# Compressed values on 32-row tiles of TensorE, and second score passes of two token blocks on separate 64-row halves

## What is computed

```
# first layer, sparse attention: 16 heads in 4 groups, head size 64; 31 compressed keys and values per group
s_c = einsum('bqgrd,bcgd->bgrqc', q, k_cmp) * scale + bias
p_c = masked_softmax(s_c, valid_c)
o_c = einsum('bgrqc,bcgd->bqgrd', p_c, v_cmp)
...
return gate0 * o_c + gate1 * o_s + gate2 * o_w      # selected and window parts beside it

# second layer, attention to the second memory: 4 heads of size 64, 256 memory tokens
sm = einsum('bshd,bmhd->bhsm', qm, km) * 64 ** -0.5
pm = softmax(sm)
o  = einsum('bhsm,bmhd->bshd', pm, vm)
```

## Time and profile before

| | |
|---|---|
| median of 3 runs | 2376.61 us (2376.5 to 2378.73) |
| span of the profiled execution | 2373.4 us |
| busy PE, PEld | 99%, 83% |
| busy DVE, ACT, POOL | 60%, 42%, 7% |
| chain that ended last | PE 96%, DVE 2%, ACT 1% |
| mean granted clock of TensorE | 0.998 |

### The profile page before, as it was taken

How to read it: one execution, slowest core, us unless ns; L and a number is a source line. 1 busy time by engine, 2 the same in 40 slices (tenths; PEclk the granted TensorE clock), 3 DMA queues, 4 the chain that set the end, 5 groups by cost and what they waited for, 6 DMA issues and landing times.

```text
span 2373.4 us, 30181 instructions
## 1 busy us (share of the span) xinstructions
PE 2350.3 (99%) x11448; PEld 1971.2 (83%) x11448; DVE 1420.6 (60%) x2891; ACT 1000.5 (42%) x1852; POOL 165.1 (7%) x251
## 2 busy tenths in 40 slices
PE   9999999999999999999999999999999999999998
PEld 7888889888888888878888888888888887888887
DVE  6434546775658897875434446677754667543444
ACT  4223335442335676653322234666523346322322
POOL 0000000110001223310000000111100001000000
PEclk9999999999999999999999999999999999999999
DMA  4455434332332211223333334211223432223322
GB/s 151 118 118 142 118 111 149 116 107 81 116 102 80 73 54 63 67 89 98 98 90 107 94 108 120 81 54 58 65 83 116 132 105 67 97 88 108 98 88 90
DMA packets 86410, 231.33 MB, mean 97 GB/s; under 512 B 8505, under 2 KB 23481, under 8 KB 86267
## 3 DMA queue, kind: packets, MB, share of 16 engines
q1 hardware_dynamic: 81072, 221.42, 29.5%
q10 hardware_dynamic: 5194, 7.98, 2.1%
HBM read 217.83 MB, written 11.53 MB: 97 GB/s over the span
## 4 chain that ended last, share of the span: by engine, by line
PE 96%; DVE 2%; ACT 1%; issue 1%; DMA 0%; POOL 0%; DVEq 0%; SPq 0%; ACTq 0%
PE bank L1136 92%; PE bank L1385 2%; PE bank L1211 1%; PE bank L1557 0%; PE bank L1232 0%; DMA t_XT<-in_xT 0%; DVE t_pp L2387 0%; DVE t_pw L2387 0%; ACT t_whi L1676 0%; DVE t_PS L2120 0%; DVE t_wlo L2115 0%; DVE t_XL L2124 0%; ACT t_pw L1829 0%; DVE t_XT L2765 0%; DVE t_PW L2120 0%
## 5 line engine op out<-in xcount | busy, mean ns | idle before, releaser
L1136 PE MATMUL bank<-t_XH,t_whi 128*128 128x512 f32 x2064 | 813.4, 394 | 0.7 <-DVE t_wlo L2115 0.5
L1136 PE MATMUL bank<-t_XL,t_whi 128*128 128x512 f32 x2064 | 804.7, 390 | 0.0
L1136 PE MATMUL bank<-t_XH,t_wlo 128*128 128x512 f32 x2048 | 799.0, 390 | 0.0
L2115 DVE TENSOR_TENSOR t_wlo<-t_raw,t_whi 128x1024 fp32r<-128x1024 f32 (+2 forms) x416 | 478.6, 1152 | 386.2 <-ACT t_whi L1676 382.8
L1676 ACT ACTIVATE t_whi<-t_raw 128x1024 fp32r<-128x1024 f32 (+3 forms) x422 | 416.9, 989 | 436.8 <-PE bank L1136 371.8
L1136 PEld LDWEIGHTS bank<-t_XH,t_whi 128*128 128x128 f32 x2064 | 388.0, 188 | 80.9 <-issue 1.6
L1136 PEld LDWEIGHTS bank<-t_XL,t_whi 128*128 128x128 f32 x2064 | 388.3, 188 | 77.1
L1136 PEld LDWEIGHTS bank<-t_XH,t_wlo 128*128 128x128 f32 x2048 | 384.8, 188 | 80.9
L1136 PE MATMUL bank<-t_RX,t_whi 128*128 128x512 f32 x1056 | 325.4, 390 | 0.0
L2243 DVE TENSOR_TENSOR t_tmp<-bank,t_RB 128x512 f32<-128x512 f32 x178 | 122.6, 689 | 198.6 <-PE bank L1136 193.3
L1136 PEld LDWEIGHTS bank<-t_RX,t_whi 128*128 128x128 f32 x1056 | 198.2, 188 | 41.0 <-issue 0.2
(11 more groups left out here) (335 smaller groups left out, 2686.9 us busy)
## 6 DMA issues: line engine op xcount, KB each, us to landing
t_raw<-in_f_in SPq DMA_DIRECT2D x86, 512.0 KB, 3.5
t_raw<-in_f_out SPq DMA_DIRECT2D x32, 384.0 KB, 3.1
t_raw<-in_w_conv SPq DMA_DIRECT2D x24, 512.0 KB, 3.5
t_raw<-in_w_merge SPq DMA_DIRECT2D x24, 512.0 KB, 3.5
t_raw<-in_fg SPq DMA_DIRECT2D x22, 512.0 KB, 3.4
t_raw<-in_fu SPq DMA_DIRECT2D x22, 512.0 KB, 3.4
t_raw<-in_f_out SPq DMA_DIRECT2D x32, 320.0 KB, 3.0
t_raw<-in_w_g SPq DMA_DIRECT2D x16, 512.0 KB, 3.5
```

The costliest lines, as they stand in the source:

```text
L1136: return e.matmul(o, l, r, start=start, stop=stop, skip_group_check=True)
L2115: e.tensor_tensor(wlo[n % NRAW][:, 0:width], raw[n % NRAW][:, 0:width], f32(whi[n % NHI][:, 0:width]), ALU.subtract).then_inc(*w_lo.tick(n))
```

## The change

1. **Compressed values.** `VC` becomes one 128-column piece: rows 32 r to 32 r + 31 hold head `r`'s values, without zeros around them. The four matmuls of a place use 32 rows each of `VC` and of `PCT`, and their order becomes: high part for both heads, then low part for both heads. The clearing of `VC` and the waits on it go.
2. **Stacked queries.** In odd blocks of tokens the halves are swapped: the high part lies in rows 64 to 127 and the low part in rows 0 to 63. `stack_q` writes even and odd blocks apart, so that each 64x512 piece becomes two pieces of 2x128 columns. This holds for all three kinds of heads.
3. **Score passes.** For `mm2` heads alone (`PAIRED`) an even tile's `score` issues only the first pass; the odd tile's `score` issues its own first pass and then both second passes, each on the 64 rows that hold the high part of the query, and a single update of the semaphore tells of both tiles. The `spa` and `win` tiles have the same passes on 128 rows as before.

```diff
+PAIRED = ('mm2',)
+def side(i):
+    return slice(64, 128) if i % 2 else slice(0, 64)
+def blocks(ap, odd):
+    return ap.rearrange("p (b o n) -> p b o n", o=2, n=P)[:, :, odd, :]
...
-    VC = place("VC", 18304, 512, F32R).rearrange("p (r n) -> p r n", r=4)
+    VC = place("VC", 18304, P, F32R)
...
         def score(t):
             hd, i = w.tiles[t]
...
+            if hd.kind != "mem":
...
+                o, q, k, i = parts = stacked_score(t)
+                mm(o, q, k[0], True, False)
...
+                    ends, begins = (hd.kind in PAIRED and i % 2 == 1), (hd.kind in PAIRED and i % 2 == 0)
+                if begins:
+                    waiting.append((t, parts))
+                    return
+                pair = [waiting.pop(), (t, parts)] if ends else [(t, parts)]
+                for _, (o, q, k, x) in pair:
+                    rows = side(x) if ends else slice(0, P)
+                    f = mm(o, q[rows], k[1][rows], False, True)
+                done = [n for n, _ in pair] + ([t + 1] if hd.kind == "spa" and i == 0 else [])
+                f.then_inc(*full.tick(*(("score", n) for n in done)))
+                return
...
-                l = QM[:, h, s]
-                mm(o, l, KM[:, h, 0, :], True, False)
-                f = mm(o, l, KM[:, h, 1, :], False, True)
...
                     operand(("pc", g))
-                    for x in range(2):
-                        f = two(banks[("out", n - 3 + 2 * x)], VC[:, r - 1 + x, :], PCT[0], PCT[1], False, True)
+                    for c in range(2):
+                        for x in range(2):
+                            rows = slice(32 * (r - 1 + x), 32 * (r + x))
+                            f = mm(banks[("out", n - 3 + 2 * x)], VC[rows, :], PCT[c][rows, :], False, c == 1)
...
             for h in range(2):
-                copy(o[0:64, h, :], ht[64 * h:64 * h + 64, :]).then_inc(*x_hi.tick(item))
+                for odd in range(2):
+                    copy(blocks(o[side(odd), h, :], odd), blocks(ht[64 * h:64 * h + 64, :], odd)).then_inc(*x_hi.tick(item))
...
-            on.wait_ge(*cleared.at("sparse"))
             for r in range(4):
-                copy(VC[32 * r:32 * r + 32, r, 0:64], f32(vch[32 * g:32 * g + 32, :])).then_inc(*x_hi.tick(("pc", g)))
+                copy(VC[32 * r:32 * r + 32, 0:64], f32(vch[32 * g:32 * g + 32, :])).then_inc(*x_hi.tick(("pc", g)))
...
-                e.tensor_tensor(o[64:128, h, :], x[s, :], ht[s, :], ALU.subtract).then_inc(*x_lo.tick(item))
+                for odd in range(2):
+                    e.tensor_tensor(blocks(o[side(1 - odd), h, :], odd), blocks(x[s, :], odd), blocks(ht[s, :], odd),
+                                    ALU.subtract).then_inc(*x_lo.tick(item))
...
-        def sparsezero():
-            on.wait_ge(*full.at(("values", 3)))
-            e.memset(f32(VC), 0.0).then_inc(*cleared.tick("sparse"))
```

More of the change, by code:

```diff
@@ L1132, in pe_program @@
         on = Once(e)
+        waiting = []
         banks.begin()
@@ L1326, in mgate, with stacked_score @@
             dense(("mgate", m), n, *X, ("n", 1))
[L1328 to L1333, removed]
-            for x in range(2):
[L1335 to L1338, removed]
+        def stacked_score(t):
+            hd, i = w.tiles[t]
+            s, wd = slice(i * P, (i + 1) * P), width(hd, i)
+            o = take("sc", ("score", t))[:, 0:256 if hd.kind == "spa" and i == 0 else wd]
+            if hd.kind == "spa":
+                g, r, a = hd.more["g"], hd.more["r"], hd.more["a"]
+                operand(("sq", g, r // 2))
+                operand(("skp", g // 2, a, g % 2))
+                if i == 0:
+                    operand(("skp", g // 2, 1, g % 2))
+                    banks.of["score", t + 1] = o[:, P:256]
+                    return o.rearrange("p (a n) -> p a n", a=2), QS[g % 2][:, r, s], [KS[:, :, g % 2, c, 0:P] for c in range(2)], i
+                return o, QS[g % 2][:, r, s], [KS[:, a, g % 2, c, 0:wd] for c in range(2)], i
+            if hd.kind == "win":
+                g, r = hd.more["g"], hd.more["r"]
+                operand(("qa", g, 1))
+                operand(("ka",))
+                k0 = max(i - 1, 0) * P
+                return o, QS2[g % 2][:, r, s], [KS2[:, g // 2, c, k0:(i + 1) * P] for c in range(2)], i
+            h = hd.more["h"]
+            operand(("mq2", h // 2))
+            operand(("mk2", h // 2))
+            return o, QM[:, h, s], [KM[:, h, c, :] for c in range(2)], i
@@ L1347, in score @@
             s = slice(i * P, (i + 1) * P)
[L1348 to L1364, removed]
[L1365 to L1376 removed]
+            h = hd.more["h"]
+            for q in range(2):
+                operand(("mq", h, q))
+                operand(("mk", h, 1))
+                Q = MQ[h % 2]
+                f = three(o, Q[0][:, q, s], Q[1][:, q, s], MK[0][:, 2 * h + q, :], MK[1][:, 2 * h + q, :], q == 0, q == 1)
             f.then_inc(*full.tick(("score", t)))
@@ L2566, in cnorm @@
             if i == 2:
-                on.wait_ge(*cleared.at("sparse"))
-                if g:
-                    on.wait_ge(*full.at(("cturn", g - 1)))
+                on.wait_ge(*full.at(("cturn", g - 1) if g else ("values", SPAH - 1)))
                 on.wait_ge(*calc.at(("cgate", g)))
```

26 lines of the change are left out of this document (10 added, 16 removed).

## The result

| | kernel before | changed kernel |
|---|---|---|
| median of 21 runs each | 2376.77 us (2376.29 to 2378.73) | 2379.77 us (2378.67 to 2382.48) |
| ratio | | 1.0013, 95% interval 1.0007 to 1.0019 |
| profiled execution, span | 2373.4 us | 2379.4 us, time 2381.24 |

A forecast was written before the change was run, and what follows sets the result against it. TensorE, busy 99%, was taken as the bound, except in `mm2`, bound by a chain through several engines. Terms -1.0 + 0.66 + 0.64 + 0.37 + 0.2 = +0.9 us gave 2377.5 us, range 2373.8 to 2381.2.

The forecast's parts named there:

- The main case: Whole kernel: the summed terms hold, +0.9 us to 2377.5 us, spanning 2375.5 to 2379.5; chance 0.60.
- the low clock: Rival in `mm2`: the stretch at clock 0.55 could last through the values at 1977.66; +3.1 us, 2379.7; chance 0.10.
- the copies: Rival in the attention stretches: half of the 5.9 us of added DVE copy time reaches PE; +3.6 us, 2380.2; chance 0.08.
- Sites, -1.0 us: Eight compressed-value sites: 32-row tiles overlap, each taking 0.86 us instead of 0.98 with two switches, gaining 0.12 each.
- Pairs in `mm2`, +0.66 us: Second memory attention: each pair dearer by 0.28 us, 0.19 at the 1.2 GHz level; three exposed pairs count in full.
- Tile 12, +0.64 us: In `mm2`, its late second pass makes DVE weigh tiles 12 and 13 back to back, delaying the value matmuls 0.64 us.
- Query copies in `mm2`, +0.37 us: Second `stack_q` call of `mm2` on DVE: four pieces instead of two delay the first weighing 0.37 us.
- The other 16 copies, +0.2 us: Calls for `spa` and `win`: 5.9 us more on DVE, of which 0.2 reaches PE, with bounds 0 and 5.9.
- Around the span: Whole kernel: the median of the runs, 2376.61 us, lies 3.2 us over the profiled span of 2373.4.
- GpSimd, nothing: The 128x512 memset and two waits on it go; GpSimd is busy 7%, so no time is gained.

The follow-up runs named there:

- one path of experiments: Parts added to the kernel before: compressed values on tiles 2375.19 us, plus swapped halves 2377.45, plus reordered score passes on 128 rows 2378.28, full change 2379.77.
- the other: The changed kernel with swapped query halves in `mm2` only, sparse and window queries written as before: 2376.8 us, 3.0 us below the changed kernel.
- extra matmuls: Matmuls whose result nobody reads, issued in TensorE's waits in `mm2`: added to the changed kernel 2378.32 us, to the kernel before with compressed values on tiles 2374.92.
- pairs on full rows: The changed kernel with its order of score passes, but second passes on all 128 rows one after the other: 2378.28 us, +1.6 against the kernel before.
- all three waits were filled: Kernel before with compressed values on tiles, unread matmuls in `mm2`, unread transposes near 930 and 1025 us, two groups moved to a free bank: 2374.37 us.
- with only the wait in `mm2` filled: Kernel before with compressed values on row tiles and 13 unread matmuls in `mm2`: 2374.92 us, -1.8 against the kernel before.
- the tiles' kernel: The kernel before with only the compressed values on 32-row tiles: 2375.19 us, -1.5 against the kernel before.
- the changed kernel with extra instructions at all places: The changed kernel with unread matmuls in `mm2` and 35 unread transposes in sparse attention: 2378.25 us, +1.4 against the kernel before.

## Why the prediction came out as it did

The change is below 0.2% and the median lies in the stated range; the forecast was 2.3 us low. The main case, given 0.60, spanned 2375.5 to 2379.5, and 2379.77 lies outside it. What held the median in the range was the room left for two rivals, the low clock (0.10) and the copies (0.08), and both came true in part. Step by step:

- **Sites, -1.0 us.** Right (tiles overlap, weights of the second pair hidden, drains at both ends). The way in costs 0.09 (0.20 instead of 0.11), and behind the site the next wide matmul follows after 0.34 instead of 0.23, both as priced. The sites gain 0.14 us each, 1.1 in all. PE's lead grows by 1.4 to 1.5 over the whole stretch, and the medians give 1.5; the 0.4 more lie outside the sites, and I had no term for them.
- **Pairs in `mm2`, +0.66 us.** The price was right at the full clock: from one pair's start to the next it is 0.745 us in the records, where four wide passes take 0.48, so 0.27 dearer; 0.28 was forecast. Where it counts was wrong. I took PE "nearly without a gap" from 1972.86 on for the bound, so that three pairs would cost in full. At the full clock they cost 0.04 us there (4.80 against 4.76), because PE has slack against the chain of the other engines. PE had looked full because part of that stretch ran at the low level. At the low level they do cost, and more than I had: I held the switches at 0.40 us while the saved stream counted double, +0.19, but four matmuls of a pair take 1.58 us there instead of 1.05, +0.53. From the first transposes to the values it is 6.05 to 6.46 us in the three profiles of the changed stage, and 4.80 before. With the clock's own effect (below) the switches cost 1.4 us.
- **Tile 12, +0.64 us.** Right: 0.66 at the full clock with the switch; +0.8 by the medians for the order alone, -0.5 when this pair is undone.
- **Query copies in `mm2`, +0.37 us.** Right: 2.59 against a forecast of 2.60.
- **The other 16 copies, +0.2 us.** This is the step that failed. They cost 1.9 us by one path of experiments (2.3, less 0.37 for the copies in `mm2`) and 3.0 by the other. I priced DVE alone and reasoned that they "lie beside dense matmuls"; of the rival I wrote that "no copy lies close before one of the long waits of PE". The copies delay ScalarE's weight copy, DVE's subtraction behind it and the weighing behind that, and PE waits for the weighing. By the starts of the same matmuls it is 0.7 us near 850 (0.59 without the tiles, 0.71 to 0.79 with them in six profiles), 0.3 near 930, 0.5 and 0.3 to 0.4 in the window, 1.9 to 2.0 us in all. That is the whole of the first path's figure; the second leaves 1.0 us, which I cannot place with certainty. A spell at the low clock behind the longer wait near 930 (1.40 instead of 1.06 us) would do it; of seven profiles with split sparse copies and no extra transposes there, six have a spell between 930 and 960, of four without such copies, two. That is not enough to call it shown.
- **The clock rival** (0.10) came true in its mechanism beside the main case: it asked whether the low clock lasts through the values, and it does; taking it away gives 1.4 us back in the medians. I had held against it that PE's wait "grows by a fifth only". What the runs leave open is why the stretch is longer with the pairs. In the profiles with pairs of the changed kernel and no extra matmuls it lasted 6.8 us (three) or 10.2 (one), with pairs on full rows 3.4, and unpaired 3.4 (three) or none (one). The switches lie in all the long ones.
- **Around the span.** I took 3.2 us between span and time. The profiled runs of the changed kernel and of the experiments show 1.75 to 2.15. So the profiled execution of the kernel before was itself about 1.4 us faster than its median; it has no spell in sparse attention. Since only differences were added to the median, the forecast did not suffer.
- **GpSimd, nothing.** Not tested by itself; nothing in the runs speaks against it.

In one line, forecast against the first path of experiments: sites -1.0 and -1.5, copies +0.57 and +2.3, late second passes +0.64 and +0.8, switches +0.66 and +1.4, sum +0.9 and +3.0. The traces give nearly the same sum by another way: -1.5, +1.9 and +0.37 for the copies, +0.7 for order and switches at the full clock, and 1.4 for the low level by the medians, +2.9. What remains open is how the loss divides between `mm2` and the other stages: the two paths give +2.6 and +1.5 for `mm2`, and the intervals don't separate them.

## What to carry to other kernels

Splitting a product over row tiles pays only where the saved stream is longer than the two changes of mode: four streams of 512 columns into two gained 0.14 us a site, two of 256 into one lost 0.27 us a pair of tiles. A copy that "only" runs on an engine with 58% idle time must be followed through that engine's queue to the next thing that the bottleneck waits for; here the layout that a 16-tile stage wanted was paid for in two other stages that got nothing from it. In a stage bound by a chain, a TensorE that looks full may be running at the low level with slack: look at the clock before pricing what one adds there, and at more than one execution. Where two kernels have the same matmuls in the same order, the difference of their starts shows each place that costs, also where the sum of the waits stands still.

## What was unexpected in the hardware

- A change of row tiles at the 1.2 GHz level: from a pair's last wide matmul to the half-row ones 0.49 us and 0.51 us out of them (1975.517, 1976.008, 1976.518 in the records); at 2.4 GHz 0.21 and 0.31. These are from start to start, with the stream of 256 columns in them.
- The rounded type runs on two row tiles at once: starts 0 to 9 ns apart over the eight sites with 32 rows, 3 to 4 ns with 64. A pair of 512 columns is followed by the next after 0.33 us, load included; two such streams one after the other take 0.46.
- Waits of TensorE can cost more behind them than they are long: 1.8 us of waits ahead of 1975.2 in the changed kernel's profile, and a stage 2.9 us longer than at the full clock (17.11 against 14.22), 1.6 and 2.2 us longer in the two other profiles of that stage. With extra matmuls inside the wait in `mm2` the clock stayed at 1.00 behind it in all five profiles; without them it fell in eight of nine.
- Short spells at the low level come and go between executions of one kernel, 1.1 to 1.6 us each, and they are a part of the scatter of its times. Where all three waits were filled, the nine runs with a mean clock of 0.999 lie within 0.4 us and the two at 0.998 are 1.2 us or more above them. It is not the whole: with only the wait in `mm2` filled the tiles' kernel scatters little too (ten of eleven runs within 0.6 us), and the changed kernel with extra instructions at all places spreads over 2.3 us at a clock of 0.999 in every run.
